# Zero products on TensorE left out of the further blocks of both expert stages

## The reference, cut to what matters

```python
# first block: 2 of 32 experts a token, width 256
e_p, e_idx = lax.top_k(jax.nn.softmax(e_logits, axis=-1), TOPK_IN_GROUP)
...
return (jax.nn.silu(xb @ w_gate[e]) * (xb @ w_up[e])) @ w_down[e]

# second block: 4 of 32 experts a token, width 1024
top_logits, top_e = lax.top_k(logits, TOP_K)
...
gu = xe @ w_gu[e] + b_gu[e]
x_glu = jnp.minimum(gu[:, :D_FF], SWIGLU_LIMIT)
x_lin = jnp.clip(gu[:, D_FF:], -SWIGLU_LIMIT, SWIGLU_LIMIT)
act = (x_lin + 1) * (x_glu * jax.nn.sigmoid(SWIGLU_ALPHA * x_glu))
return act @ w_dn[e] + b_dn[e]
```

## Time and profile before

| | |
|---|---|
| median of 3 runs | 1959.06 us (1958.43 to 1960.88) |
| the profiled execution | 1958.97 us, span 1957.4 us |
| TensorE matmuls (PE) | 1777.1 us busy, 91% |
| VectorE / ScalarE | 564.1 us / 394.2 us, 29% / 20% |
| mean granted TensorE clock | 0.976 of 2.4 GHz |
| DMA | 626.69 MB, mean 320 GB/s, 428 GB/s at the plateau |
| stage one / stage two | about 390 to 670 us / about 974 to 1948 us |

### The profile page before, as it was taken

The page is one execution under the profiler, slowest core; times in us unless marked ns, Lnnn a source line. Parts: engine busy times, 40 slices in busy tenths (PEclk is TensorE's granted clock), DMA queues, the critical chain, the costliest instruction groups (busy, mean ns, idle before and its releaser), DMA issues.

```text
span 1957.4 us, 26971 instructions
## 1 busy us (share of the span) xinstructions
PE 1777.1 (91%) x10656; PEld 981.4 (50%) x10657; DVE 564.1 (29%) x1279; ACT 394.2 (20%) x908; POOL 49.4 (3%) x111
## 2 busy tenths in 40 slices
PE   7999999986687899999989999899898999989987
PEld 4766778764454668678733333333333333333332
DVE  4685331221121346442421111111111111111112
ACT  3244551120111411442301111011110111100111
POOL 0040000000000002000000000000000000000000
PEclk9999999998898999999999999999998999999999
DMA  9977113349999648214556999999999799999996
GB/s 397 419 268 298 66 65 125 119 194 413 425 425 422 266 154 346 87 44 137 232 234 256 428 428 428 428 428 428 427 428 428 291 428 428 428 428 428 428 427 282
DMA packets 59256, 626.69 MB, mean 320 GB/s; under 512 B 7136, under 2 KB 11232, under 8 KB 16832
## 3 DMA queue, kind: packets, MB, share of 16 engines
q1 hardware_dynamic: 53440, 603.24, 74.6%
q0 software_dynamic: 5456, 21.11, 2.9%
q10 hardware_dynamic: 272, 1.05, 0.1%
HBM read 624.32 MB, written 1.05 MB: 319 GB/s over the span
## 4 chain that ended last, share of the span: by engine, by line
PE 58%; DMA 34%; DVE 3%; issue 3%; ACT 2%; DVEq 1%; SPq 0%; ACTq 0%
PE ps L512 55%; DMA ring<-in_w_gu_dram 27%; DMA ring<-in_moe_w_gate_dram 4%; PE ps L680 2%; DMA ring<-in_w_dn_dram 1%; DMA ring<-in_moe_w_down_dram 1%; ACT arena L1550 1%; DMA hN<-in_x_dram 1%; ACT arena L1718 0%; DVE stat L2117 0%; DVEq L1992 0%; DVE arena L2134 0%; SPq L537 0%; DVE hN L2007 0%; DVE rstd L1963 0%
## 5 line engine op out<-in xcount | busy, mean ns | idle before, releaser
L512 PE MATMUL ps<-ring,arena 128*64 128x512 f32 (+2 forms) x4288 | 721.7, 553 | 95.4 <-DMA ring<-in_w_gu_dram 48.5
L512 PEld LDWEIGHTS ps<-ring,arena 128*64 128x64 f32 (+1 forms) x4288 | 236.6, 129 | 528.3 <-issue 409.4
L512 PE MATMUL ps<-arena 128*32 128x256 f32 (+13 forms) x2434 | 385.7, 456 | 45.4 <-issue 19.2
L512 PEld LDWEIGHTS ps<-arena 128*64 128x64 f32 (+8 forms) x2434 | 172.8, 147 | 231.5 <-issue 161.0
L512 PE MATMUL ps<-hT,ring 128*128 128x256 f32 (+1 forms) x960 | 234.5, 399 | 4.0 <-ACT hT L1550 1.6
L512 PEld LDWEIGHTS ps<-hT,ring 128*128 128x128 f32 x960 | 178.5, 190 | 58.7 <-issue 35.6
L2383 DVE TENSOR_SCALAR arena<-ps 128x512 f32<-128x512 f32 (+1 forms) x34 | 23.0, 676 | 514.7 <-PE ps L512 514.7
L1550 ACT ACTIVATE arena<-ps 128x512 f32<-128x512 f32 (+4 forms) x189 | 103.5, 571 | 284.3 <-PE ps L512 152.4
L1813 ACT ACTIVATE arena<-ps,mod,gain 128x128 f32<-128x128 f32 x176 | 66.1, 458 | 420.5 <-PE ps L512 420.5
L1825 ACT ACTIVATE arena<-arena 128x512 f32<-128x512 f32 (+1 forms) x44 | 25.3, 575 | 571.6 <-DVE arena L2383 383.1
L512 PEld LDWEIGHTS ps<-arena,hN 128*128 128x128 f32 x896 | 105.0, 194 | 31.5 <-issue 17.0
(11 more groups left out here) (313 smaller groups left out, 939.8 us busy)
## 6 DMA issues: line engine op xcount, KB each, us to landing
ring<-in_w_gu_dram SPq DMA_DIRECT2D x96, 2048.0 KB, 25.5
ring<-in_w_dn_dram SPq DMA_DIRECT2D x64, 2048.0 KB, 21.4
arena<-in_w_gu_dram SPq DMA_DIRECT2D x32, 2048.0 KB, 27.3
ring<-dense_dram SPq DMA_DIRECT2D x56, 1024.0 KB, 7.4
ring<-in_moe_w_up_dram SPq DMA_DIRECT2D x16, 2048.0 KB, 17.5
ring<-in_moe_w_down_dram SPq DMA_DIRECT2D x16, 2048.0 KB, 16.0
ring<-in_ada_w_dram SPq DMA_DIRECT2D x24, 1024.0 KB, 18.9
ring<-in_moe_w_gate_dram SPq DMA_DIRECT2D x8, 2048.0 KB, 21.4
```

Source lines behind the costliest of these rows:

```text
L512: ins = nc.tensor.matmul(*a, start=start, stop=stop, **k)
```

## The change

The six calls of `occupy` in the two `further` functions go. Nothing else changes, on no other engine either. The calls outside of `further` stay, those of the first blocks' surroundings too.

```diff
@@ moe1, further
-                    occupy(7, 6, True)
                     pe.wait_ge(s["ys"], p + 1)
                     pe.wait_ge(x["gather_onehot"], q + 1)
                     gather_group(x, ohgM)
-                    occupy(7, 7, True)
                     pe.wait_ge(x["xs"], q * 2 + 2)
                     hidden_group(it, u, x, xsM1, False)
                     pe.wait_ge(x["spread_onehot"], q + 1)
                     spread_turn(x, ohsM, 3, T)
-                    occupy(7, 4, True)
                     pe.wait_ge(x["act"], q + 1)
                     act_turn(2, x)
@@ moe2, further
-                    occupy(7, 9, True)
                     pe.wait_ge(s["ys"], e + 1)
                     pe.wait_ge(x["gather_onehot"], q + 1)
                     gather_strips(x, ohgM)
                     pe.wait_ge(x["rows"], q + 1)
                     strips_turn(x)
-                    occupy(7, 4, True)
                     pe.wait_ge(x["xs"], q + 1)
                     hidden_strips(it, u, x, xsM)
-                    occupy(7, 7, True)
                     pe.wait_ge(x["act"], q + 1)
                     act_turn(2, x)
```

## The result

The kernel got slower: 1970.9 us in the median of five runs (1968.65 to 1972.99), against 1959.9 of the kernel before in its five (1958.43 to 1961.06). The ratio is 1.0057 with the interval [1.0043, 1.0072], so +11.0 us. The forecast had been 1963.4 us, with a range to 1967.0: the sign was right, the size was not. The profiled execution took 1972.99 us, span 1971.4, mean granted clock 0.968.

The account below looks back on a forecast made before the run. The prediction took weight transfers to bound most of both expert stages, with TensorE's gains or losses in the further blocks moving the end along. Terms 0.9 + 1.2 + 2.3 + 0 = +4.4 us on 1958.97 gave 1963.4 us, range 1958.4 to 1967.0.

Parts of the forecast that it names:

- A: Stage one's first further block: gather starts earlier, -0.5 us; clock falls after idle, +1.4; together +0.9 us.
- B: Stage one's second further block: clock may fall before the down products, half the price taken, +1.2 us, bounds 0 and 2.6.
- C: Stage two's first further block: clock falls before the dense hidden products, nearly certain, +2.3 us, bounds 0 and 4.5.
- D: Stage two's second further block: waits for weights absorb the loss, 0 us, bounds -0.5 and +1.
- Rival 2: Further blocks: the clock falls twice or longer, sum +7.8 us, some 1967.5 us with D's +1; chance 0.12.
- Rival 1: Further blocks: the clock holds, only the earlier gather counts, -0.5 us, 1958.5 us; chance 0.25.
- Theory 2: Whole kernel, set against the result for the follow-up runs: all 11 us are the clock; no chance given.
- Rival 3: Jump at stage two's start: shorter code changes its 4.83 us stand by -3 to +0.6 us; chance 0.04, clock held.

Follow-up runs that it names:

- e3: Kernel before with the zero products removed in stage two's further blocks only: 1962.45 us against 1961.22, ratio 1.0012.
- e5: Kernel before, all zero products kept, with 94 one-column products (188 instructions) at the start: 1962.7 us against 1961.22, ratio 1.0007.
- e13: Kernel before, all zero products kept, with 40 one-column products (80 instructions) at the start: 1960.74 us against 1961.47, ratio 0.9995.
- e4: Changed kernel with 34 one-column products (68 instructions) at the start: 1959.3 us against 1961.22 of the kernel before, ratio 0.9989.
- e14: As e13, but the further blocks' zero products have one column each: 1970.23 us against 1961.47 of the kernel before, ratio 1.0043.
- e1: Kernel before with each zero product of the further blocks replaced by a one-column product, same code length: 1965.13 us against 1961.22, ratio 1.0026.
- e9: Changed kernel with 44 one-column products (88 instructions) at the start: 1959.08 us, ratio 1.0003 to the kernel before.
- e7: Kernel before without stage one's 6 and 7 zero products, the other zero products kept, 30 one-column products at the start: 1976.2 us against 1959.78, ratio 1.0082.
- e11: As e7, with 35 one-column products at the start instead of 30: 1958.21 us against 1962.27 of the kernel before, ratio 0.9979.

## Why the prediction was wrong, step by step

*A, +0.9.* The earlier start came as worked out, 0.65 us. The price behind it was right in size, 1.7 for the 1.4 taken. But the three profiles of before put A at 28.3 in the mean and not at 29.4: the gather's fall, which I took for part of the state before, happened in one of three (with e3, e5 and e13 in three of six, A at 28.6). Measured against that, A costs +2.4, or about +2. The term was too small because its base was one execution. Nor is the price behind it fixed: e4 runs A's code of after and has 28.7, with no second fall.

*B, +1.2.* +1.7, inside the bounds: a fall at both the gather and the down products. The 1.6 us lost at the gather went into the wait for the weight, 2.90 us before and gone now; the 1.7 at the down products stayed.

*C, +2.3.* +2.0 in after, and 9.0 us for the hidden products, as the prediction had asked for. In e14 it was +5.2, with a second fall at the down products (5.25 and not about 3.7 us): the upper bound of 4.5 can be reached and passed.

*D, 0.* -0.9, a little below the lower bound of -0.5: the loss is absorbed by the waits for weights, as forecast, and the down products run somewhat better.

The four terms together are +5.2 against 4.4. That they come so near is in part luck, since A lies 1.5 above its term and D 0.9 below. With equal code, e1 gives +5.1 for the clock, and e14 against e13 +9.4, in another place. (Rival 2's sum was 0.3 off: 1958.97 + 7.8 + 1 is 1967.8, not 1967.5.) Rival 1 (the clock holds, 0.25) is refuted: the hidden products of C take 9.0 us in after and no less in e1. The Trainium skill (TensorE: Matmul & The Clock Gate, "Why this matters for your kernels") asks for idle gaps below some 3 us; the falls here came behind gaps of 1.98, 2.29 and 1.08 us (rows 406.47, 631.38 and 1031.49, the last with 2.26 and 0.53 in front of it), so the trace does not agree with it as a safe bound.

*The step that failed* is the one that isn't in the sum. The prediction said that the plateau is bound by DMA and moves along with the blocks, and so gave the loop of stage one nothing. It named the sign of this itself, an end that moves by more than the four blocks do: 11.0 us against 5.2. In before it does run at the transfers' rate, 424 GB/s, but with nothing in hand: TensorE already stood 52 to 54 us of its 200 us on "issue", and the earlier trace rows show two of these stands. Some 5 us more of them freed the slots later, as SyncE's rows show, and the rate fell to 413. Shortening the code inside of the loop by 68 instructions moved, as I read it, where its jumps land against the transfers of code. The middle went up by 7.0 us, 5.0 of them in such stands; code at the old length in the old place (e1) takes it back, and code at the new length in another place (e4, e9) more than back, with all zero products still gone. Theory 2 falls with e4, e9 and e7: in e7 the clock's cover is better than in after, and by the ratios it is 5 us slower (the intervals touch).

Rival 3 had the mechanism and the wrong place. It priced one jump, at the start of stage two, between -3 and +0.6 us. That one didn't move (4.85 for 4.83 us). The loop takes its two jumps three times, and there the nearest rows, 3.28 and 5.43, were no bound for a second stand of 5.2 behind the first, nor for a jump back that costs from nothing (e4) to 18.4 us (e7).

What stays open: what decides whether the loop is kept. With 1765 instructions (counted from their order, which may be off by some ten, while the differences between kernels are exact; before has 1833) it is kept at shifts of 68 and 88, not at 0 and 40; with 1781 at 80, nearly at 70, not at 60; with 1833 not at 0, 80 and 188. The runs give no rule that fits all of these. It is not settled, nor why a stand lasts 5 us or 17.

## What to carry to other kernels

Removing instructions that cost nothing on the path is no neutral edit when they lie in a loop's body, even in a branch that most turns skip: look for "issue" behind jumps in the profile of before, add up these stands over all turns, and take that total as the uncertainty of the sum. Test such a change at two or three shifts of the code (a few empty products at a place where the engine waits anyway) before the change itself gets the blame: here the shift alone is worth up to 20 us, the clock 5 to 9. And where a term rests on a fallen or a full clock behind a gap of about 2 us, profile before more than once.

## What the runs showed of the hardware

A loop of 1765 or 1781 instructions on TensorE can run from code that stays on the chip: 43 code transfers and 3.0 us of "issue" (e4), against 69 to 71 transfers and 52 to 71 us where every turn fetches anew. Stage two's loop has 16 turns and is kept in every kernel: 3 transfers from 1000 to 1948 us in before, 3 to 6 in all the others. The Trainium skill (Runtime: NRT & Kernel Launch, "Instruction fetch mechanics") says that code comes in blocks of 16 KiB, 256 instructions, that TensorE's buffer holds 2048 of them, and that a taken branch to code outside the window waits; the size of a transfer (1.13 MB / 69 = 16 KB) agrees, and the stands agree in kind. As an estimate from the page's 256, a loop of 1765 is 6.9 blocks long and one of 1833 is 7.2, and the number of blocks that it touches would be a candidate for what decides; the last turn of e11, at 7.0, doesn't fit it plainly. The page also says that prefetch is purely sequential and that no instruction cache helps, with a window of two pages. The 43 transfers of e4 don't agree with that: its jumps back over the whole loop need no new code.

With the weights streaming at more than 410 GB/s, a stand lasted 3 to 6 us at the inner jump and 9.4 to 18.4 us at the jump back; no run shows what it would be with the queues idle. The clock's answer to nearly the same gap differs between executions of the same kernel: 3.73 or 5.24 us for A's gather behind 2.03 to 2.06 us of idle and six zero products.
